# Two layers of a hybrid network on one core: loads, bias table, head norms, rotation, values and doubled keys moved into the first product chain

## The reference

```python
h = concatenate([meta, x])
# layer 0
hn = _rmsnorm(h, norm_attn[0])
qa, ka, va, qb, kb, vb = jnp.split(hn @ w_in_even, EVEN_SPLITS, axis=-1)   # 512 512 512 | 512 128 128
lam = exp(sum(lv[0]*lv[1])) - exp(sum(lv[2]*lv[3])) + lam_init
oa = _diff_attention(qa, ka, va, lam, table, pos)        # bias of each (query, key) from rel_table
qb = _rmsnorm(qb per head of 64, qk_norm[0]); kb = _rmsnorm(kb per head of 64, qk_norm[1])
qb, kb = _axial_rope(qb, ...), _axial_rope(kb, ...)
ob = _gqa_dense(qb, kb, vb)                              # 8 query heads share 2 key heads
# layer 1
qc, kc, vc = jnp.split(_rmsnorm(h, norm_attn[1]) @ w_in_odd, ODD_SPLITS, axis=-1)   # 1024 | 128 | 128
oc = _window_gqa(qc, kc, vc, sinks, table)
```

## Time and profile before

| what | us |
|---|---|
| median of 3 runs | 4104.45 (4101.89 to 4107.82) |
| the profiled execution | 4099.06, its span 4097.2 |
| from the start to the first instruction of attention A | 208.69 |
| from the start of chain `qk1` (first PE instruction 824.52) to attention C | 91.3 |
| PE busy, share of the span | 3783.7 (92%) |
| DVE, ACT, POOL busy | 1854.9, 1196.2, 175.8 |

### The profile page before, as it was taken

How to read it: one execution, slowest core, us unless ns; L and a number is a source line. 1 busy time by engine, 2 the same in 40 slices (tenths; PEclk the granted TensorE clock), 3 DMA queues, 4 the chain that set the end, 5 groups by cost and what they waited for, 6 DMA issues and landing times. The chain is left out here.

```text
span 4097.2 us, 51286 instructions
## 1 busy us (share of the span) xinstructions
PE 3783.7 (92%) x20561; PEld 3123.6 (76%) x20561; DVE 1854.9 (45%) x2503; ACT 1196.2 (29%) x1767; POOL 175.8 (4%) x214
## 2 busy tenths in 40 slices
PE   6877999989999978999999989998899999998997
PEld 6755999985788856876887868876686688777885
DVE  3365534325544234356555443333435664454333
ACT  2144312215322134223223232214423222323222
POOL 0000000000000000000330000000000033000000
PEclk9888999988999989999999999999999999999998
DMA  2100222211222220221002222221122100222222
GB/s 107 47 22 21 93 89 86 83 64 28 90 95 94 91 77 22 102 83 62 1 1 78 93 72 87 103 77 63 42 84 91 52 1 1 98 72 92 98 86 84
DMA packets 49634, 279.93 MB, mean 68 GB/s; under 512 B 10453, under 2 KB 13533, under 8 KB 20197
## 3 DMA queue, kind: packets, MB, share of 16 engines
q1 hardware_dynamic: 49434, 277.13, 19.3%
HBM read 274.80 MB, written 2.27 MB: 68 GB/s over the span
## 5 line engine op out<-in xcount | busy, mean ns | idle before, releaser
L334 PE MATMUL ps<-xs,ffn_w 128*128 128x512 f32 x2112 | 483.4, 392 | 29.5 <-DVE xs L599 29.5
L334 PEld LDWEIGHTS ps<-xs,ffn_w 128*128 128x128 f32 x2112 | 399.2, 189 | 114.2 <-issue 31.1
L334 PE MATMUL ps<-u,mlp_w 128*128 128x264 f32 (+1 forms) x2880 | 456.2, 321 | 14.8 <-DVE mlp_w L593 10.0
L334 PEld LDWEIGHTS ps<-u,mlp_w 128*128 128x128 f32 x2880 | 417.3, 190 | 53.3 <-issue 15.5
L334 PE MATMUL ps<-hn,mlp_w 128*128 128x264 f32 (+1 forms) x2304 | 363.7, 320 | 0.0
L334 PEld LDWEIGHTS ps<-hn,mlp_w 128*128 128x128 f32 x2304 | 332.5, 188 | 30.3 <-issue 0.5
L334 PE MATMUL ps<-xs,cv_w 128*128 128x512 f32 x1152 | 278.1, 402 | 8.6 <-DVE cv_w L593 8.6
L334 PEld LDWEIGHTS ps<-xs,cv_w 128*128 128x128 f32 x1152 | 218.5, 191 | 75.0 <-issue 23.2
L334 PE MATMUL ps<-ff,ffn_w 128*128 128x512 f32 x1056 | 240.0, 389 | 0.0
L381 ACT CAST ffn_w<-raw 128x2048 fp32r<-128x2048 f32 (+1 forms) x74 | 124.0, 1676 | 383.2 <-PE ps L334 343.2
L334 PEld LDWEIGHTS ps<-ff,ffn_w 128*128 128x128 f32 x1056 | 198.3, 188 | 41.1
(11 more groups left out here) (413 smaller groups left out, 5334.3 us busy)
## 6 DMA issues: line engine op xcount, KB each, us to landing
raw<-in_w_ffn_up SPq DMA_DIRECT2D x44, 1024.0 KB, 4.7
raw<-in_w_up SPq DMA_DIRECT2D x32, 1024.0 KB, 4.7
raw<-in_w_down SPq DMA_DIRECT2D x32, 1024.0 KB, 4.8
raw<-in_w_conv SPq DMA_DIRECT2D x24, 1024.0 KB, 4.7
raw<-in_w_ffn_down SPq DMA_DIRECT2D x32, 704.0 KB, 4.0
raw<-in_w_mqk SPq DMA_DIRECT2D x10, 1024.0 KB, 4.8
raw<-in_w_mv SPq DMA_DIRECT2D x8, 1024.0 KB, 4.7
raw<-in_w_mo SPq DMA_DIRECT2D x8, 1024.0 KB, 4.8
```

What stands on the lines that cost most here:

```text
L334: ins = nc.tensor.matmul(bank(u)[:, h, :], w[:, s, wp, k * g.bw + j * P:k * g.bw + (j + 1) * P], g.xs[:, xp, k, h * n:(h + 1) * n], start= ...
```

## The change

The stages `ld1`, `lam`, `rel`, `vp0`, `qkn`, `rope` and `vp1` are gone as stages, and their functions with them, apart from `row_norm` and `load_all`, which others use.

The even chain has now two products over the same `hn`: `plain`, 10 tiles (B's queries 4, its two key heads on one tile, values 5), and `maps`, 8 tiles (A's queries and keys), 18 in all. Values come out as features and are turned to tokens by PE transposes (`turn`), copied by ACT (`copy_turned`). The doubled key tiles are made by three ACT copies (`double`). The odd chain has 10 tiles as before: keys 1, values 1, queries 8.

Both chains are called with `tiles=3`, so three pairs of PSUM banks serve the tiles and the fourth (banks 6 and 7) serves the work beside them. Their blocks are written out and not looped.

`Start` issues the loads in this order: weight block 0, table, buckets, `par`, `h` in eight transfers by chunk (constants `mats` after the second), weight block 1, `vecs`, `cs`, `sinks`. It also does the table and `lam`. `EvenHeads` does head norm (squares and root on ACT, a full 128 by 528 reciprocal on DVE, group sums by a product with a block matrix) and rotation for five tiles, one step between two tiles of the chain. `attend` places some of its buffers in `qk` (`spare`); its order is as before.

```diff
-def chain(nc, ps, ws, name, gemms, whole=None, gain=None, squares=None, room=None, beside=None):
+def chain(nc, ps, ws, name, gemms, whole=None, gain=None, squares=None, room=None, beside=None, tiles=TILES, whole_in=None):
...
+        g.unroll = TILES // g.tpb if tiles == TILES else g.n_blocks
+        g.m0 = sum(f.tiles for f in gemms[:gemms.index(g)])
...
-            return tile_no(g, pos * g.tpb + j, pos > 0) % TILES
+            return tile_no(g, pos * g.tpb + j, pos > 0) % tiles
...
                         ins.then_inc(filled, 1)
+                        if beside is not None and isinstance(b, int):
+                            beside.between(pe, g.m0 + b * g.tpb + j)
...
-                    u = (g.t0 + g.tpb) % TILES
+                    u = (g.t0 + g.tpb) % tiles
...
                     for c in range(cuts[q], cuts[q + 1]) if whole is not None else ():
+                        if whole_in is not None:
+                            act.wait_ge(whole_in[c], 16)
...
+    def sync(self, sp):
+        ws, s = self.ws, self.s
+        dram, row = ws.one[0][0]
+        ws.load(sp, dram, row, 0, 0, ws.first_in[0])
+        sp.dma_start(self.tab[0:BUCKETS, :], self.a["rel_table"]).then_inc(s["table_in"], 16)
+        sp.dma_start(self.hot[:, :, :], self.a["buckets"]).then_inc(s["table_in"], 16)
+        self.send(sp, "par")
+        for c in range(KC):
+            sp.dma_start(self.h[:, c, :], self.a["xT"][:, c, :]).then_inc(self.h_in[c], 16)
+            if c == 1:
+                self.send(sp, "mats")
+        ws.load(sp, dram, row, 1, 1, ws.first_in[1])
+        for name in ("vecs", "cs", "sinks"):
+            self.send(sp, name)
...
+    def tensor(self, pe, n):
+        if n == -1:
+            w = REL_N // 3
+            pe.wait_ge(self.s["table_in"], 32)
+            pe.wait_ge(self.s["ones_set"], 1)
+            for i in range(6):
+                v, part = divmod(i, 3)
+                self.nc.tensor.matmul(self.ps[0:REL_HEADS, 2 + i, 0:w], self.tab[:, :], self.hot[:, v, part * w:(part + 1) * w],
+                                      start=True, stop=True).then_inc(self.s["filled"], 1)
+            pe.wait_ge(self.loaded["mats"], 16)
...
+    def vector(self, dve, n):
+        nc, s, dots, lam = self.nc, self.s, self.dots, self.lam
+        if n == -1:
+            nc.vector.memset(self.tab[BUCKETS:BUCKETS + 1, :], 1.0).then_inc(s["ones_set"], 1)
...
+class EvenHeads(Doubled):
...
+    def between(self, pe, m):
+        if m == 3:
+            self.sums(pe, 0)
+        if m in (4, 6, 8, 10):
+            self.sums(pe, m // 2 - 1)
+        if m in (5, 7, 9, 11, 13):
+            self.rotate(pe, (m - 5) // 2)
+        if m == 12:
+            pe.wait_ge(self.s["times_sin"], 4)
+            self.turn(pe, 0, self.g, 5)
...
+                            plain = Dense("plain", hn, KC, 2, 1280, "scale", dst=qk[:, 8:18, :], inv=root_of(L))
+                            maps = Dense("maps", hn, KC, 2, D, "scale", dst=qk[:, 0:8, :])
...
+                product = Dense("qk", hn, KC, 2, 1280, "scale", dst=qk[:, 0:10, :], inv=root_of(L))
+                chain(nc, ps, ws, "qk1", [product], beside=OddHeads(nc, ps, product, v, qk[:, 10, :], ident), tiles=3)
```

More of the change, by code:

```diff
@@ L275, in chain @@
             beside.open(st)
+            beside.banks_freed(freed, lambda g, t: tiles + tile_no(g, t, t >= g.tpb) + 1)
         with nc.Block() as block:
@@ L989, in _, with attend @@
                         low(nc.gpsimd, c)
[L992 to L1030 removed]
+def attend(nc, ps, name, qk, v, mix, mix_meta, ident, jobs, room, scratch=None, sinks=None, lam=None, spare=None):
     NJ = len(jobs)
@@ new lines, with turn, copy_turned, double @@
+class Doubled(Beside):
+    def turn(self, pe, j, g, t):
+        nc, ps, s = self.nc, self.ps, self.s
+        pe.wait_ge(self.freed, self.taken(g, t))
+        nc.tensor.transpose(ps[0:META, 7, 0:P], g.dst[:, t, 0:META], self.ident)
+        for c in range(SEQ // P):
+            ins = nc.tensor.transpose(ps[:, 6, c * P:(c + 1) * P], g.dst[:, t, META + c * P:META + (c + 1) * P], self.ident)
+        ins.then_inc(s["v_turned"], 1)
+    def copy_turned(self, act, j):
+        nc, ps, s = self.nc, self.ps, self.s
+        act.wait_ge(s["v_turned"], j + 1)
+        nc.scalar.copy(self.v[0:META, 0, j * P:(j + 1) * P], ps[0:META, 7, 0:P])
+        nc.scalar.copy(self.v[:, 1:NT, j * P:(j + 1) * P], ps[:, 6, :].rearrange("p (c n) -> p c n", c=NT - 1)).then_inc(s["v_copied"], 1)
+    def double(self, act, a, b):
+        nc, s = self.nc, self.s
+        nc.scalar.copy(b[0:HD, :], a[HD:P, :]).then_inc(s["doubled"], 1)
+        nc.scalar.copy(b[HD:P, :], a[HD:P, :]).then_inc(s["doubled"], 1)
+        act.wait_ge(s["doubled"], 2)
+        nc.scalar.copy(a[HD:P, :], a[0:HD, :])
@@ new lines, with __init__, open, between @@
+class OddHeads(Doubled):
+    def __init__(self, nc, ps, g, v, last, ident):
+        self.nc, self.ps, self.g, self.v, self.last, self.ident = nc, ps, g, v, last, ident
+    def open(self, st):
+        self.s = {x: st.sem("head_" + x) for x in "v_turned v_copied doubled".split()}
+    def between(self, pe, m):
+        if m == 3:
+            self.turn(pe, 0, self.g, 1)
+    def scalar(self, act, n):
+        if n == 2:
+            act.wait_ge(self.freed, self.taken(self.g, 0))
+            self.double(act, self.g.dst[:, 0, :], self.last)
+            self.copy_turned(act, 0)
@@ new lines, with __init__, open, banks_freed @@
+class Together(Beside):
+    def __init__(self, *parts):
+        self.parts = parts
+    def open(self, st):
+        for part in self.parts:
+            part.open(st)
+    def banks_freed(self, freed, taken):
+        for part in self.parts:
+            part.banks_freed(freed, taken)
+    def sync(self, sp):
+        for part in self.parts:
+            part.sync(sp)
+    def gpsimd(self, pool):
+        for part in self.parts:
+            part.gpsimd(pool)
+    def tensor(self, pe, n):
+        for part in self.parts:
+            part.tensor(pe, n)
+    def between(self, pe, m):
+        for part in self.parts:
+            part.between(pe, m)
+    def scalar(self, act, n):
+        for part in self.parts:
+            part.scalar(act, n)
+    def ahead(self, dve, n):
+        for part in self.parts:
+            part.ahead(dve, n)
+    def vector(self, dve, n):
+        for part in self.parts:
+            part.vector(dve, n)
@@ L1597, in first_block @@
 def first_block(nc, ps, ws, a, x2):
-    starts, sizes = [0] + [META + P * t for t in range(4)], [META] + [P] * 4
-    qk_f, v_f = 1792, 640
+    v_f = 640
     with ExitStack() as ctx:
@@ L1610, in first_block @@
         sinks = sb("sinks", [P, C_HEADS])
[L1611 to L1616 removed]
+        vecs = room[:, 2 * L + 2 * REL_N:2 * L + 2 * REL_N + 4 * HD].rearrange("p (j n) -> p j n", j=4)
+        lam, gain_a = sb("lam", [P, 1]), sb("gain_a", [P, 1])
+        ident, ones, rot, blocks = (mats[:, j, :] for j in range(4))
         def parts(name, chunks, n=L):
@@ L2626, in program @@
         gates_in = ctx.enter_context(nc.semaphore("gates_in"))
-        with nc.Block() as block:
-            @block.sync
-            def _(sp):
-                ws.send_first(sp, *ws.one[0][0])
         first_block(nc, ps, ws, a, x)
```

411 lines of the change are left out of this document (200 added, 211 removed).

## The result

The changed kernel takes 4035.7 us (median of 4 runs, 4028.6 to 4040.5), the kernel before beside it 4103.2 (4098.4 to 4107.8). The ratio is 0.9834, with a 95% interval of 0.9815 to 0.9854: 67.5 us less, where the prediction had 69.6. The profiled execution took 4033.35 us with a span of 4031.6; before it was 4099.06 and 4097.2, so the spans differ by 65.6 us.

What follows compares the result with a forecast made beforehand. PE, busy 92% of the span, and its order in the two chains were taken as the path. Savings of 48.5 and 21.1 us, 69.6 together, from the median 4104.45 gave 4034.9, rounded to 4035; 8-in-10 range 4020 to 4055.

Steps and rivals of the forecast that it cites:

- The start: First stage: the table's matmuls wait for DVE's prologue, PE idle until 20.4 us, first product 27.7, first block ends 41.0.
- The first rival: Start: row of ones there in time, table from 8 to 15 us, 14.5 us less, total 4020; chance 0.08.
- The wait for pair 0: Behind the sum of squares, both chains: the next tile waits until tile 0 is emptied, PE idle 4.9 us.
- Its clock: Behind the wait for pair 0: clock falls to the lower level, 1.5 us lost per chain.
- The steps between tiles: Even chain: ten head matmul pairs at 1.05 us and five sets of transposes at 0.83 add 14.65 us.
- the rival of a chain at the lower level: Even chain never reaches the upper clock: 5.9 us more per tile, 94 us over 16 tiles, total 4129; chance 0.03.
- The sixteen tiles: Even chain, the tiles left after the first block and the wait: 94.4 us.
- No hand-off late: Even chain: all ten hand-offs hide with 4.5 to 5.7 us to spare; rival of late ones: 4067, chance 0.08.
- The end of the even chain: Last tile to attention A: last copy 0.9 us and clearing 13 semaphores 1.8 us, so attention A starts at 160.2.
- The odd layer: Odd chain ends at 893.65, attention C starts at 894.7 instead of 915.8: 21.1 us less.
- Outside both parts: All other stages: nothing counted; 0 to 1 us for PE's higher clock entering the attentions, taken as 0.
- Slow chunks: Rival: the eight loads of `h` come at 165 GB/s, prologue ends 3 to 4 us later, total 4039; chance 0.07.

Runs made afterwards that it cites:

- ones_early: The changed kernel with the table's row of ones set by GpSimd at the start, not by DVE behind its prologue: 4021.2 us, ratio 0.9794.
- squares_apart: The changed kernel with the sum of squares of both chains in the fourth pair of banks, taking no tile number: 4018.2 us, ratio 0.9788.
- filled_wait: The changed kernel with eight useless PE products behind each sum of squares, in the wait for pair 0: 4030.5 us, ratio 0.9821.
- h_in_one: `ones_early` with `h` loaded in one transfer instead of eight, and the matrices behind it: 4029.5 us, ratio 0.9811.

## Why the prediction held, and where its steps were off

- **The start** came as written, 0.9 us late: first part of `h` on ACT at 8.08 and split at 8.85 (8.2 forecast), DVE's prologue done at 20.98 (20.35), table at 21.27 for 7.21 us (20.4, 7.25), first block at 28.41 for 13.29 us (27.7, 13.30). The reading of DVE's order, that the memset stands behind the prologue, decided it, and `ones_early` showed what hung on it: 13.1 us up to attention A. The first rival, which assumed the row in time, gave 26.5 for the sum of squares; it came at 28.15 when that was made true.
- **The wait for pair 0**: idle 5.11 us in both layers, 4.9 forecast from before's root, reciprocal and emptying. `squares_apart` removed it.
- **Its clock**: 1.5 us forecast, by likeness to the idle time ahead of `qk1`. Measured 1.9 in the even layer (13.67 us from 47.70 to 61.37, against two tiles of 5.87, my estimate of a plain tile: the 70.81 us of the earlier trace rows, without what the last record reaches past the next start, over twelve) and 2.1 in the odd. `filled_wait` ties it to the idle time. By the Trainium skill ("TensorE: Matmul & The Clock Gate", Part 1) the lower clock is the default state; the trace agrees, in that PE came out of 5.11 us of idle time at the lower level. Of the two levels (1.2 and 2.4 GHz) the windows behind the wait show the lower for some 4 us, and then the upper (PEclk is the third column from the right):

```profile
44.00:48.00 4.00, 0.30 (x1) 0.34 (x2) 3.96 (x3) 2.97 (x4) 0.00 (x0) 0.62 0.10 21
48.00:52.00 4.00, 4.00 (x20) 4.00 (x20) 2.46 (x2) 0.84 (x2) 0.00 (x0) 0.52 0.16 20
52.00:56.00 4.00, 4.00 (x35) 4.00 (x35) 0.30 (x1) 0.00 (x0) 0.00 (x0) 1.00 0.60 242
```

- **The steps between tiles** were the term most mis-sized. I took ten head steps at 1.05 and five sets of transposes at 0.83: 14.65 us. By the starts they add about 0.87 and 0.57 (6.74 and 6.44 less 5.87), 11.5 in all, 3.1 less. No change of the clock is in this: PEclk was 0.98 over the whole stretch with the 4 us at the lower level in it, so the rival of a chain at the lower level did not come either. A record of a matmul ends after the next has begun; what a group adds is the distance from start to start. The sixteen tiles then took 93.9 (94.4).
- **No hand-off late**: no idle time of PE between 47.70 and 155.19, so the longer code cost nothing there, and 3.45 us more of DVE in each round brought no wait.
- **The end of the even chain**: 155.19 to 158.12, 2.9 us for the last copy and 13 semaphores, 2.7 forecast. Together attention A at 158.1, forecast 160.2: 50.6 us less, forecast 48.5.
- **The odd layer**: 20.0 us less, forecast 21.1. The first block took 13.7 and not 13.3, the wait 0.2 more, its clock 0.6 more, the transposes 0.3 less.
- **Outside both parts** I counted nothing, with 0 to 1 us for the clock at the attentions' entries. Attention A took 3.0 us more and `mlp0` 1.0, which I did not look into; with `subln` and the rest it is 5.0. This is the step of the sum that failed: the same instructions of attention A took from 106.9 to 112.6 us in the profiles above, and 1 us was too tight a bound for it.

That the forecast of 4035 met 4035.7 to within 1 us is luck. The mechanism was right, and the two parts together came to 70.6 us where 69.6 was forecast, with +2.1 in the even layer and -1.1 in the odd. But the profiles differ by 65.6 us and not by 69.6, for the 5.0 us outside. The medians differ by 67.5, and the median of the kernel before came out 1.3 us lower beside the changed kernel (4103.17) than the one that I subtracted from (4104.45): 2.1 us too much gain and 1.3 us too high a start cancel. The interval of the ratio alone is 8 us either way.

**Slow chunks** did not come: the first 21.3 us moved data at 286 GB/s, near the window of 302 that I went by the earlier trace rows. The Trainium skill ("DMA: Bandwidth & Descriptors", Measured) advises transfers of 1 MiB or more. The trace of `h_in_one` agrees in the small: the whole of `h` came 0.2 to 1.1 us sooner in one piece. For this kernel the measurement decides against it, since the sum of squares came 3.3 us later.

## What to carry to other kernels

When work is moved beside other work, look for the smallest instruction that the moved work still waits for, and at what stands ahead of it in its engine's queue: a memset of 0.07 us behind 12 us of DVE cost 13 us. When a ring of buffers gets one place fewer, write down for each tile which place it takes, the odd ones out (here a sum of squares) among them: the wait of 5.1 us was in that list, 2 us of clock came with it, and a place that stood free removed them. And count steps of PE by their distance from start to start, not by their records.

## What the hardware showed that I had not expected

- The clock column reads 1.00 in the first stage although PE ran slowly there. In `h_in_one` the first 30 products of the block took 6.68 us, 223 ns each, and the last 54 took 6.88, 127 ns each, with 1.00 in the column for both. In the changed kernel, where all splits were ready, the first 10 products took the 2.0 us from 28.4 to 30.4 and 19 took those from 32.4 to 34.4, with 1.00 too:

```profile
14.70:21.40 6.70, 6.69 (x31) 6.20 (x30) 6.70 (x11) 6.70 (x13) 0.00 (x0) 1.00 0.28 102
24.75:31.40 6.65, 6.65 (x54) 6.65 (x55) 3.22 (x8) 3.74 (x4) 0.00 (x0) 1.00 0.44 156
```

  Here, behind PE's idle start, the column is no proof of the upper level; the time of a known product is.
- The same instructions of one stage, in which PE works in pieces with waits between them, took 106.9 to 112.6 us in kernels that differ ahead of it, 5%, and 110.8 and 112.6 in two executions of one kernel. This is more than many changes bring; whether what stands ahead sets it is not shown.
- 3.7 us of useless products in a wait made the way behind it shorter: from the sum of squares to the end of tile 3 it was 18.0 us with them (41.91 to 59.92) and 19.8 with PE at rest (41.53 to 61.37).
